# One projection call for the first token mixer, with most of the modulation beside it

## The chip, the cores and the metric

The kernel runs on 1 core of one Trainium2 chip. The metric is the device time of one execution in microseconds. One execution of each kernel is also profiled, and its trace gives the rows shown here. TensorE (PE) multiplies and transposes, VectorE (DVE) and ScalarE (ACT) work elementwise, GpSimd (POOL) does one elementwise job in the part that is changed, and all transfers of this part are issued from one queue, SyncE's (SP).

## The reference, cut to what matters

Two transformer blocks follow each other; the change touches only the first token mixer, up to the residual that follows it. All is float32, with 512 tokens, 256 context tokens and a model width of 1024.

```python
mod = (silu(c) @ w_ada + b_ada)                       # w_ada: 1024 x 6144
sh_mix, sc_mix, g_mix, sh_ffn, sc_ffn, g_ffn = split(mod, 6)
mod_ctx = silu(c_ctx) @ w_ada[:, :2 * d] + b_ada[:2 * d]
h = modulate(rms_norm(x, norm_mix_g), sh_mix, sc_mix)
p_in = h @ w_in + b_in                                # w_in: 1024 x 5824
u = gelu(p_in[..., U]); v = gelu(p_in[..., V])
tq = axial_rope(p_in[..., TQ]); tk = axial_rope(p_in[..., TK]); tv = p_in[..., TV]
nq, nk, nv = ...                                      # 16 heads of 32
gate_a = sigmoid(p_in[..., GA]); gate_b = sigmoid(p_in[..., GB])
hc = modulate(rms_norm(ctx, norm_mix_g), mod_ctx[:d], mod_ctx[d:])
# the context's own tk, tv, nk, nv come from hc and the same columns of w_in
tiny = tiny_attention(tq, tk, tv, tk_c, tv_c) @ tiny_w_o
o_a = u * (mix_in_chunks(layer_norm(v)) + tiny)
o_b = neighbourhood_attention(nq, nk, nv, nk_c, nv_c, na_rpb, rows)
merged = gate_a * (o_a @ w_up_a) + gate_b * (o_b @ w_up_b)
x = x + g_mix * (merged @ w_out)
```

## The kernel before, in words

The program is a sequence of blocks (`nc.Block()`): in each, every engine has its own list of instructions, and the next block starts when all engines are through. Within a block, semaphores set the order. There is no planner: the order of the lists is the order of the work. `linked` makes an engine wait for its own last result.

The order is this. `load_constants` brings the identity, the packed columns, two gate rows and `x`. `modulation` multiplies both silu vectors by `w_ada` in 12 blocks of 512 columns (3 buffers; 8 fp32 matmuls with a 512-wide moving operand per block, L208; ScalarE copies the row out, L198), turns the rows into columns, makes the gains and shifts, and spreads the two gate rows over the partitions (L218, L244); one gate row goes to DRAM. `first_mixer` loads `ctx`, norms the 6 row tiles of `x` and `ctx` (`normalise`: squares on ScalarE L266, root, scaling on VectorE L281), turns them into `hT` (`turn`), loads the bias row, and calls `project`.

`project` multiplies in three passes of a split format: each weight block, two buffers, comes in two halves of its rows; ScalarE rounds a half to its high part (L486), VectorE subtracts it for the low part (L500), and TensorE does hi x hi, hi x lo, lo x hi (L452). A unit is one PSUM tile of 24 such matmuls, there are 4 tiles, and each unit is written out by the engine that it names, in order. On VectorE and ScalarE, block b + 1 is halved before the units of block b are written out. SP issues the weights of block b when block b - 2 is done. `side` gives pieces of other work to an engine, placed after the units of a block; before the change only other callers use it.

The first call covers `v`, `tiny` (the small q, k, v), `nq`, `nk` and `nv`, mostly in blocks of 512 columns. Then `joined` adds the halves of `hT` back, since the low half was written over it. The next block prepares: gelu of `v` and its layer norm, the rotations of the small queries and keys, and on GpSimd the bias planes (`near_bias`, L1009, three operations). Then follow a `turn`, `attend` (the tiny attention, four strips), `near_attention` (the windowed attention), a second `project` for `u` (with `hT` halved again), the mixing (`ps_sgu`, L1098 to L1112, whose weights are loaded at its start), a third `project` for both gates in blocks of 256 columns, `merge`, and the output projection with the residual. After that come the experts, the second mixer and the second feed-forward, which the change leaves alone but for where the gate row of the experts' residual is read.

Of the kernel before, what the change touches and what calls it, by code (L numbers as in the profile page):

```python
# [21 lines left out]
P = 128  # L22
# [123 lines left out]
def load_constants(core, a, keep):  # L146

    nc = core.nc
    loads = [(keep["ident"][:], a["k_ident"]), (keep["cols"][:], a["cols"]),
             (keep["gate_mix_row"][:], a["b_gates"][0:D].partition_broadcast(P)),  # L150
             (keep["gate_ffn_row"][:], a["b_gates"][D:2 * D].partition_broadcast(P)),
             (keep["x"][:], a["x"].rearrange("(t p) d -> p t d", p=P))]
    done = core.sig("constants_in")
    with nc.Block() as block:
        @block.sync
        def _(sp):
            for dst, src in loads:
                sp.dma_start(dst, src).then_inc(done.sem, 16)
            sp.wait_ge(done.sem, 16 * len(loads))


def modulation(core, a, keep, scratch):
# [3 lines left out]
    NB, W = 6 * D // W_BLOCK, W_BLOCK  # L166
    w = core.sb("w_ada", [P, 3, KD, W])
    silu_c = core.sb("silu_c", [P, KD, 2])
    rows = core.sb("mod_rows", [2, 6 * D])
    first = core.sb("first_row", [2, P])  # L170
    mod = core.sb("mod", [P, 6 * KD, 2])
    w_in = [core.sig(f"ada_w_{i}") for i in range(3)]
    first_in, c_ready, mm, row_ready = (core.sig(n) for n in ("first_row_in", "silu_c_ready", "ada_mm", "mod_row_ready"))
    turned, row_mm, chain, row_out = (core.sig(n) for n in ("mod_turned", "gain_row_mm", "dve_chain", "gain_row_out"))
    c0 = COLS["c"][0]
    col = keep["cols"]
    with (core.psum("ps_mod_rows", [2, 2, W], F32) as ps, core.psum("ps_mod", [P, 6 * KD, 2], F32) as ps_mod,
          core.psum("ps_row", [P, 2, 2 * W], F32) as ps_row, nc.Block() as block):
        @block.sync
        def _(sp):  # L180
            for b in range(NB):
                if b >= 3:
                    sp.wait_ge(mm.sem, b - 2)
                sp.dma_start(w[:, b % 3], dram_rows(a["w_ada"], b * W, (b + 1) * W)).then_inc(w_in[b % 3].sem, 16)
                if b == 0:
                    sp.dma_start(first[:], a["k_first"]).then_inc(first_in.sem, 16)
            sp.wait_ge(row_out.sem, 4)
            sp.dma_start(scratch["gate_row"], keep["gate_ffn_row"][0:1, :]).then_inc(core.sig("gate_row_kept").sem, 16)

        @block.scalar  # L190
        def _(act):

            for j in range(2):
                nc.scalar.activation(silu_c[:, :, j], col[:, c0 + j * KD:c0 + (j + 1) * KD], ACT.Silu) \
                    .then_inc(c_ready.sem, 1)
            for b in range(NB):
                act.wait_ge(mm.sem, b + 1)
                nc.scalar.activation(rows[:, b * W:(b + 1) * W], ps[:, b % 2, :], ACT.Copy).then_inc(row_ready.sem, 1)  # L198

        @block.tensor  # L200
        def _(pe):
            pe.wait_ge(c_ready.sem, 2)
            for b in range(NB):
                pe.wait_ge(w_in[b % 3].sem, 16 * (b // 3 + 1))
                if b >= 2:
                    pe.wait_ge(row_ready.sem, b - 1)
                for k in range(KD):
                    last = nc.tensor.matmul(ps[:, b % 2, :], silu_c[:, k, :], w[:, b % 3, k, :], start=k == 0,  # L208
                                            stop=k == KD - 1)
                last.then_inc(mm.sem, 1)  # L210
            pe.wait_ge(row_ready.sem, NB)
            for n in range(6 * KD):
                last = nc.tensor.transpose(ps_mod[:, n, :], rows[:, n * P:(n + 1) * P], keep["ident"][0:2, 0:2])
            last.then_inc(turned.sem, 1)
            pe.wait_ge(first_in.sem, 16)
# [2585 lines left out]
```

## Time and profile before

| | us |
|---|---|
| Median of 3 runs | 4338.49 |
| The runs | 4321.89, 4339.66, 4338.49 |
| Profiled execution | 4325.14 |
| Its span in the trace | 4323.4 |
| TensorE, VectorE, ScalarE, GpSimd busy | 3868.5, 2436.8, 1742.3, 682.5 |
| Start of `merge` (its first transfer) | 755.13 |

Times in the trace are microseconds from the start of the span. In a timeline row stand the start, the length, the engine, the line, the operation with its output and inputs and the shape, the count, and in brackets how long the engine had been idle and what ended that. Rows with a count above one are merged. In a table of stretches stand, after start:end, the length, the busy time of TensorE, its weight loads (PEld), VectorE, ScalarE and GpSimd with their numbers of instructions, the clock granted to TensorE (1.00 is 2.4 GHz, 0.50 is 1.2), and the busy share and rate of DMA. An fp32 matmul of the program is two records.

### The profile page before, as it was taken

The numbers are of one execution on the slowest core, as the hardware profiler recorded it, in microseconds if no ns is written. First come the engines' busy times: TensorE is split into PE (matmuls) and PEld (weight loads), VectorE is DVE, ScalarE is ACT, GpSimd is POOL, SyncE is SP. The second block draws the span as 40 slices with busy tenths as digits, with TensorE's granted clock in tenths as the row PEclk, the third lists the DMA queues.
The fourth block names the chain that finished last, engine by engine and source line by source line (L and its number), as shares of the span: only waits on it lengthen the run. The fifth ranks groups of instructions, "written<-read, shape, count | busy, mean of one in ns | idle before, by whom it ended". The sixth has DMA issues, their size and how long they took to land. (4 is left out here: it accounts for less than half of the span.)

```text
span 4323.4 us, 46785 instructions
## 1 busy us (share of the span) xinstructions
PE 3868.5 (89%) x18351; PEld 3127.2 (72%) x18351; DVE 2436.8 (56%) x3808; ACT 1742.3 (40%) x2078; POOL 682.5 (16%) x390
## 2 busy tenths in 40 slices
PE   7694989867999999993987998799999999999999
PEld 1583867645878887882876766688888887888887
DVE  0326422546888888884336653499666643444444
ACT  0222422224888888883222331333333332222222
POOL 0002000003766776750000000000000000000000
PEclk9795779978999999995998879899999999999999
DMA  7211012224777777772212102244455455555554
GB/s 263 72 49 41 1 51 78 97 113 162 251 243 252 253 255 259 247 255 92 80 50 64 39 25 75 82 137 132 132 180 195 180 195 181 195 193 192 192 192 174
DMA packets 253046, 640.03 MB, mean 148 GB/s; under 512 B 48455, under 2 KB 147531, under 8 KB 209820
## 3 DMA queue, kind: packets, MB, share of 16 engines
q1 hardware_dynamic: 208460, 598.02, 39.4%
q0 software_dynamic: 44368, 39.01, 4.2%
q8 instruction: 147, 2.41, 0.2%
q14 instruction: 71, 0.58, 0.0%
HBM read 671.93 MB, written 125.33 MB: 184 GB/s over the span
## 5 line engine op out<-in xcount | busy, mean ns | idle before, releaser
L1541 DVE TENSOR_TENSOR w_lo<-w_raw,w_hi 128x2048 fp32r<-128x2048 f32 x288 | 653.3, 2290 | 122.8 <-ACT w_hi L1450 113.6
L1450 ACT ACTIVATE w_hi<-w_raw 128x2048 fp32r<-128x2048 f32 x288 | 544.2, 1920 | 65.7 <-DMA w_raw<-in_e_w,over_rows 62.4
L2450 DVE TENSOR_TENSOR w_lo<-w_raw,w_hi 128x2048 fp32r<-128x2048 f32 x128 | 293.4, 2293 | 351.5 <-ACT w_hi L2387 351.0
L2387 ACT ACTIVATE w_hi<-w_raw 128x2048 fp32r<-128x2048 f32 x128 | 245.5, 1918 | 522.1 <-DMA w_raw<-in_peer_u 275.4
L1165 PE MATMUL ps_peer<-peer_xT_hi,w_hi 128*128 128x512 f32 x1024 | 408.3, 399 | 5.0 <-DVE w_lo L2450 4.8
L1165 PE MATMUL ps_peer<-w_hi,coef_hi 128*128 128x512 f32 x1024 | 399.3, 390 | 5.2 <-DVE coef_lo L2547 5.2
L1167 PE MATMUL ps_peer<-peer_xT_hi,w_lo 128*128 128x512 f32 x1024 | 399.5, 390 | 0.0
L1166 PE MATMUL ps_peer<-peer_xT_lo,w_hi 128*128 128x512 f32 x1024 | 399.5, 390 | 0.0
L1166 PE MATMUL ps_peer<-w_lo,coef_hi 128*128 128x512 f32 x1024 | 399.1, 390 | 0.0
L1167 PE MATMUL ps_peer<-w_hi,coef_lo 128*128 128x512 f32 x1024 | 399.1, 390 | 0.0
L1681 PE MATMUL ps_gu<-w_hi,h2T_hi 128*128 128x512 f32 x792 | 321.4, 406 | 0.7 <-DVE w_lo L1541 0.7
L1683 PE MATMUL ps_gu<-w_hi,h2T_lo 128*128 128x512 f32 x792 | 313.0, 395 | 0.0
L1682 PE MATMUL ps_gu<-w_lo,h2T_hi 128*128 128x512 f32 x792 | 312.8, 395 | 0.0
L486 ACT ACTIVATE w_hi<-w 128x1024 fp32r<-128x1024 f32 (+5 forms) x116 | 145.3, 1259 | 377.7 <-DMA w<-in_w_in 257.7
L500 DVE TENSOR_TENSOR w_lo<-w,w_hi 128x1024 fp32r<-128x1024 f32 (+5 forms) x116 | 169.6, 1473 | 214.1 <-ACT w_hi L486 213.6
L1414 POOL DMA_INDIRECT expert_rows<-block_out,slot_token x95 | 214.9, 2262 | 131.0 <-ACT block_out L1470 62.0
L1165 PEld LDWEIGHTS ps_peer<-w_hi,coef_hi 128*128 128x128 f32 x1024 | 192.7, 188 | 45.7 <-issue 5.6
L1165 PEld LDWEIGHTS ps_peer<-peer_xT_hi,w_hi 128*128 128x128 f32 x1024 | 192.9, 188 | 43.9 <-DVE w_lo L2450 6.2
L1167 PEld LDWEIGHTS ps_peer<-peer_xT_hi,w_lo 128*128 128x128 f32 x1024 | 192.6, 188 | 40.7
L1166 PEld LDWEIGHTS ps_peer<-w_lo,coef_hi 128*128 128x128 f32 x1024 | 192.8, 188 | 40.1
L1167 PEld LDWEIGHTS ps_peer<-w_hi,coef_lo 128*128 128x128 f32 x1024 | 192.6, 188 | 40.0
L1166 PEld LDWEIGHTS ps_peer<-peer_xT_lo,w_hi 128*128 128x128 f32 x1024 | 193.0, 188 | 37.8
(487 smaller groups left out, 7736.4 us busy)
## 6 DMA issues: line engine op xcount, KB each, us to landing
w_raw<-in_e_w SPq DMA_DIRECT2D x195, 1024.0 KB
w_raw<-in_peer_u SPq DMA_DIRECT2D x64, 1024.0 KB, 5.9
w_raw<-in_peer_v SPq DMA_DIRECT2D x64, 1024.0 KB, 4.9
acts<-act_out SPq DMA_DIRECT2D x64, 512.0 KB, 6.6
gates<-gate_tile SPq DMA_DIRECT2D x8, 4096.0 KB, 15.9
act_back<-acts SPq DMA_DIRECT2D x64, 512.0 KB, 5.8
gates_back<-gates SPq DMA_DIRECT2D x64, 512.0 KB, 7.0
w<-in_w_in SPq DMA_DIRECT2D x26, 1024.0 KB, 7.3
```

The lines of the kernel that those rows point to most:

```text
L500: nc.vector.tensor_tensor(half_of(w_lo, b, half), half_of(w, b, half), half_of(w_hi, b, half).bitcast(F32), ALU.subtract) \
L1165: nc.tensor.matmul(out, w_hi, x_hi, start=first, stop=False)
L1166: nc.tensor.matmul(out, w_hi, x_lo, start=False, stop=False)
L1167: return nc.tensor.matmul(out, w_lo, x_hi, start=False, stop=last)
L1414: nc.gpsimd.indirect_dma_start(out=scratch["expert_rows"], out_offset=bass.IndirectOffsetOnAxis(ap=tok[:, r:r + 1], axis=0), in_=ob[:, b % ...
L1450: nc.scalar.activation(w_hi[:, slot(n), :], w_raw[:, slot(n), :], ACT.Copy).then_inc(hi_done.sem, 1)
L1541: nc.vector.tensor_tensor(w_lo[:, slot(n), :], w_raw[:, slot(n), :], w_hi[:, slot(n), :].bitcast(F32), ALU.subtract).then_inc(lo_done.sem, 1)
L1681: nc.tensor.matmul(out, s_hi, m_hi, start=first, stop=False)
L1682: nc.tensor.matmul(out, s_hi, m_lo, start=False, stop=False)
L1683: return nc.tensor.matmul(out, s_lo, m_hi, start=False, stop=last)
L2387: nc.scalar.activation(w_hi[:, n % 2, :], w[:, n % 2, :], ACT.Copy).then_inc(w_hi_done.sem, 1)
L2450: nc.vector.tensor_tensor(w_lo[:, n % 2, :], w[:, n % 2, :], w_hi[:, n % 2, :].bitcast(F32), ALU.subtract) \
```

## The change

- `front` replaces `load_constants`, `modulation` and the norms: SP issues the columns, then the first four blocks of `w_ada` (shifts and scales of the mixer) with `x`, the identity and `ctx` between them, each block into its own buffer. The squares and scalings stand between the row copies. Only 16 columns are turned.
- The other eight blocks of `w_ada` become 32 late steps, side work of the projection: VectorE multiplies two 128x512 pieces of `w_ada` by the silu column of their rows and adds them up in SBUF; after four steps TensorE sums over the partitions with four small matmuls against ones. The gates leave as columns, are turned, and go through DRAM to become rows.
- One call of `project` with 23 blocks, nearly all 256 columns wide: `v` 0 to 3, `tiny` 4, `nk` 5 and 6, `nv` 7 and 8, `nq` 9 and 10, `u` 11 to 14, the gates 15 to 22. `joined`, the preparing block and two of the three calls are gone. Gelu, layer norm and rotations are side pieces.
- Transfers: the first `turn` issues bias row, table and layer norm's bias; the second issues `near_mask` and `raw_bias` ahead of what follows; `near_attention` issues the mixing's weights; `x` is dropped after the first turn and loaded again beside the mixing.
- GpSimd makes the bias planes beside the tiny attention (`attend`) instead of beside the layer norm.

```diff
+N_EARLY = 4
+N_LATE = 6 * D // W_BLOCK - N_EARLY
+LATE_STEPS = KD // 2
+def front(core, a, keep, ctx, xn, silu_c):
...
+            sp.dma_start(col[:], a["cols"]).then_inc(cols_in.sem, 16)
+            ada(0)
+            sp.dma_start(x[:], a["x"].rearrange("(t p) d -> p t d", p=P)).then_inc(x_in.sem, 16)
+            sp.dma_start(keep["ident"][:], a["k_ident"]).then_inc(ident_in.sem, 16)
+            ada(1)
+            sp.dma_start(ctx[:], a["ctx"].rearrange("(t p) d -> p t d", p=P)).then_inc(ctx_in.sem, 16)
+            for b in range(2, N_EARLY):
+                ada(b)
...
+            row_copy(0)
+            act.wait_ge(x_in.sem, 16)
+            for i in range(TC):
+                if i == T:
+                    row_copy(1)
+                    act.wait_ge(ctx_in.sem, 16)
+                ins = nc.scalar.activation(junk[:], sources[i], ACT.Square, accum_out=stat[:, 0, i:i + 1])
...
+            for b in range(2, N_EARLY):
+                row_copy(b)
...
 def project(core, blocks, halve=(), side=None):
...
                 for half in range(2):
                     sp.dma_start(half_of(w, b, half), half_src(b, half)).then_inc(w_in[b % NW][half].sem, 16)
+                for piece in beside("sp", b):
+                    piece(sp, lambda b: evicted(sp, b))
...
                 last.then_inc(mm.sem, 1)
+                if n == len(units) - 1 or units[n + 1][0] != b:
+                    for piece in beside("pe", b):
+                        piece(pe, lambda b: evicted(pe, b))
...
 def attend(core, tiles, dv, outs, beside=None):
...
+        @block.gpsimd
+        def _(pool):
+            if beside:
+                beside(pool)
...
+    def fetch_late(i):
+        def piece(sp, ready):
+            b, k = divmod(i, LATE_STEPS)
+            if i >= 2:
+                sp.wait_ge(late_used.sem, i - 1)
+            at = (N_EARLY + b) * W_BLOCK
+            sp.dma_start(w_late[:, i % 2], dram_rows(a["w_ada"], at, at + W_BLOCK)[:, 2 * k:2 * k + 2]) \
+                .then_inc(late_in[i % 2].sem, 16)
+        return piece
+
+    def add_late(i):
+        def piece(dve, link, ready):
+            b, k = divmod(i, LATE_STEPS)
+            dve.wait_ge(late_in[i % 2].sem, 16 * (i // 2 + 1))
+            if k == 0 and b >= 2:
+                dve.wait_ge(late_mm.sem, b - 1)
...
+            for j in range(2):
+                src, by, to = w_late[:, i % 2, j, :], silu_c[:, 2 * k + j, 0:1], acc[b % 2][:]
+                if k == 0 and j == 0:
+                    ins = nc.vector.tensor_scalar(to, src, by, None, ALU.mult)
+                else:
+                    ins = nc.vector.scalar_tensor_tensor(to, src, by, to, ALU.mult, ALU.add)
+                if j == 0:
+                    link(ins)
+            ins.then_inc(late_used.sem, 1)
+            dve.wait_ge(late_used.sem, i + 1)
+        return piece
+
+    def sum_late(b):
+        def piece(pe, ready):
+            pe.wait_ge(late_used.sem, LATE_STEPS * (b + 1))
+            for c in range(W_BLOCK // P):
+                last = nc.tensor.matmul(ps_late[:, b * (W_BLOCK // P) + c, :], acc[b % 2][:, c * P:(c + 1) * P], ones[:],
+                                        start=True, stop=True)
+            last.then_inc(late_mm.sem, 1)
+        return piece
...
+    FIRST = 3
+    side = {"sp": {}, "act": {}, "dve": {}, "pe": {}}
+    for i in range(N_LATE * LATE_STEPS):
+        b = FIRST + i // 2
+        side["sp"].setdefault(b + 1, []).append(fetch_late(i))
+        side["dve"].setdefault(b, []).append(add_late(i))
+        if i % LATE_STEPS == LATE_STEPS - 1:
+            side["pe"][b + 1] = [sum_late(i // LATE_STEPS)]
+    side["sp"][7].append(fetch_gain)
+    side["act"][5] = [gelu_rows(t) for t in range(T)]
+    side["act"][9] = [ln_root]
+    for b, pieces in ((5, [tiny_rope(t, 0) for t in range(T)]), (6, [tiny_rope(t, TINY) for t in range(T)]),
+                      (7, [ln_moments(0), ln_moments(1)]), (8, [ln_moments(2), ln_moments(3)]),
+                      (11, [ln_centre(0), ln_centre(1)]), (12, [ln_centre(2), ln_centre(3)]),
+                      (13, [ln_gained(0), ln_gained(1)]), (14, [ln_gained(2), ln_gained(3)]),
+                      (15, [ln_shifted(0), ln_shifted(1)]), (16, [ln_shifted(2), ln_shifted(3)])):
+        side["dve"][b] += pieces
+    side["dve"][21] = [late_out]
+    with core.psum("ps_late", [P, 4 * KD, 2], F32) as ps_late:
+        project(core, blocks, [h], side)
...
+    def fetch_bias(sp):
+        sp.dma_start(mask[:], a["k_near_mask"]).then_inc(raw_in.sem, 16)
+        sp.dma_start(raw[:], a["k_rpb"]).then_inc(raw_in.sem, 16)
...
+    near_attention(core, nq, nk, nv, near_bias, onT, fetch_mixing)
...
         @block.sync
         def _(sp):
-            sp.dma_start(ws[:], a["sgu_w"]).then_inc(in_.sem, 16)
-            sp.dma_start(wo[:], a["tiny_w_o"]).then_inc(in_.sem, 16)
-            sp.dma_start(bs[:], a["sgu_b"].partition_broadcast(P)).then_inc(in_.sem, 16)
+            sp.wait_ge(rows_kept.sem, 16)
+            sp.dma_start(x[:], a["x"].rearrange("(t p) d -> p t d", p=P)).then_inc(x_in.sem, 16)
+            sp.dma_start(gate_mix_row[:], scratch["gate_rows"][0].partition_broadcast(P)).then_inc(x_in.sem, 16)
+            sp.wait_ge(x_in.sem, 32)
```

## Rows read from the trace of the kernel before

**Rows 1.** Stages: start:end, length, PE, PEld, DVE, ACT, POOL busy, clock, DMA, GB/s.

```profile
0.00:122.30 122.30, 96.60 (x248) 22.95 (x248) 3.92 (x12) 8.64 (x15) 0.20 (x4) 0.95 0.67 233
122.30:154.60 32.30, 8.50 (x48) 7.98 (x48) 10.80 (x17) 13.13 (x23) 0.00 (x0) 0.61 0.15 52
154.60:320.40 165.80, 153.11 (x816) 133.01 (x816) 43.48 (x38) 40.06 (x36) 0.00 (x0) 0.94 0.20 69
320.40:374.10 53.70, 0.00 (x0) 0.00 (x0) 46.77 (x78) 6.67 (x7) 22.57 (x4) 0.54 0.20 81
374.10:383.40 9.30, 6.77 (x38) 6.26 (x39) 3.17 (x5) 3.01 (x6) 0.00 (x0) 0.73 0.00 0
383.40:408.20 24.80, 21.27 (x100) 14.13 (x101) 11.72 (x40) 7.66 (x21) 0.00 (x0) 0.79 0.00 0
408.20:559.90 151.70, 147.88 (x1040) 128.08 (x1040) 68.41 (x172) 65.68 (x160) 0.00 (x0) 0.74 0.00 1
559.90:616.80 56.90, 45.34 (x192) 37.11 (x192) 16.03 (x12) 20.34 (x21) 0.00 (x0) 0.88 0.21 74
616.80:658.10 41.30, 32.13 (x80) 18.23 (x80) 11.13 (x16) 0.00 (x0) 0.00 (x0) 0.52 0.12 32
658.10:755.10 97.00, 89.55 (x384) 73.62 (x384) 19.61 (x16) 28.63 (x33) 0.00 (x0) 0.94 0.28 87
```

**Rows 2.** Whom TensorE waited for, 0 to 755 us: total, times, longest.

```profile
PE ps_turn L314 <- PEq L995: 54.5, 1, 54.5
PE ps_unit L452 <- DVE w_lo L500: 34.8, 3, 15.0
```

**Rows 3.** Timeline of TensorE, modulation and first turn.

```profile
21.70 85.48 PE L208 MATMUL ps_mod_rows<-w_ada,silu_c 128*2 128x512 f32 x192 [21.70 <-DMA w_ada<-in_w_ada]
141.36 8.53 PE L314 MATMUL ps_turn<-ident,xn 128*128 128x128 f32 x48 [22.37 <-PEq L260]
```

**Rows 4.** DMA issues: KB each, median us to landing.

```profile
w_ada<-in_w_ada SPq DMA_DIRECT2D x12, 2048.0 KB, 8.0
raw_bias<-in_k_rpb SPq DMA_DIRECT2D x1, 3072.0 KB, 11.5
```

**Rows 5.** Timeline of VectorE and ScalarE, evictions of the first projection.

```profile
184.41 0.69 DVE L942 TENSOR_TENSOR v<-ps_unit,b_rows 128x512 f32<-128x512 f32 x1 [4.75 <-PE ps_unit L452]
231.14 0.36 DVE L942 TENSOR_TENSOR tiny_qkv<-ps_unit,b_rows 128x192 f32<-128x192 f32 x1 [2.97 <-PE ps_unit L452]
266.75 1.23 ACT L967 ACTIVATE nk<-ps_unit,cols 128x512 f32<-128x512 f32 x1 [2.61 <-PE ps_unit L452]
269.62 0.48 ACT L948 ACTIVATE nk<-ps_unit,cols 128x256 f32<-128x256 f32 x1 [1.64 <-PE ps_unit L452]
```

**Rows 6.** Timeline of VectorE and ScalarE, gate blocks and start of merge.

```profile
695.47 1.22 DVE L500 TENSOR_TENSOR w_lo<-w,w_hi 128x1024 fp32r<-128x1024 f32 x1 [0.21 <-ACT w_hi L486]
699.79 0.69 ACT L948 ACTIVATE gate_a<-ps_unit,cols 128x512 f32<-128x512 f32 x1 [3.78 <-PE ps_unit L452]
760.65 2.50 DVE L494 TENSOR_TENSOR x_lo<-near_outT,x_hi 128x512 fp32r<-128x512 f32 x4
```

**Rows 7.** Timeline of TensorE, windowed attention.

```profile
486.19 1.04 PE L813 MATMUL ps_o<-nv,probsT 128*128 128x32 f32 x8
```

**Rows 8.** Timeline of VectorE and GpSimd, layer norm beside the bias planes.

```profile
346.98 0.60 DVE L1038 TENSOR_SCALAR ln_stats<-ln_stats 128x4 f32<-128x4 f32 x1
348.08 7.29 DVE L1043 TENSOR_SCALAR v<-v,ln_stats 128x1024 f32<-128x1024 f32 x1
L1009 POOL TENSOR_TENSOR near_bias<-near_mask,raw_bias x3: 7287/7296/7737, 340.3 to 354.8; 128x4096 f32<-128x4096 f32 x3
```

**Rows 9.** Timeline of VectorE, tiny attention.

```profile
386.05 0.21 DVE L670 TENSOR_SCALAR maxima<-maxima 128x1 f32<-128x1 f32 x1
```

**Rows 10.** Busy time in two stretches of windowed attention; columns as in rows 1.

```profile
409.90:485.00 75.10, 73.97 (x362) 62.19 (x362) 23.84 (x63) 24.14 (x59) 0.00 (x0) 0.50 0.00 1
556.70:559.90 3.20, 1.11 (x4) 0.71 (x4) 1.95 (x3) 0.00 (x0) 0.00 (x0) 0.50 0.00 0
```

More of the change, by code:

```diff
@@ L155, in _ @@
         @block.sync
         def _(sp):
[L157 to L162, printed above, removed]
-    nc = core.nc
[L166 to L188, printed above, removed]
@@ L286, in normalise, with turn @@
     core.drop(stat, junk)
-def turn(core, jobs, loads=()):
+def turn(core, jobs, loads=(), begin=None):
     nc = core.nc
@@ L300, in _ @@
         def _(sp):
+            if begin:
+                begin(sp)
             for dst, src in loads:
@@ L459, in ready @@
             def ready(b):
[L460 to L462 removed]
+                evicted(eng, b)
             halve_block(0)
@@ L924, in first_mixer @@
-    core.drop(ctx)
+    xn = core.sb("xn", [P, TC, D], high=True)
+    front(core, a, keep, ctx, xn, silu_c)
+    jobs = []
+    for k in range(KD):
+        for first, count, c0, j in ((0, T, 0, 0), (T, CTX // P, S, 1)):
+            jobs.append(([(xn[:, first + i, k * P:(k + 1) * P], i * P) for i in range(count)],
+                         scaled(nc, hT[:, k, c0:c0 + count * P], P, count * P, keep["gain_mix"][:, j, k:k + 1],
+                                keep["shift_mix"][:, j, k:k + 1])))
@@ new lines, in columns, with two @@
+    def columns(at, b, units):
+        blocks.append((dram_rows(a["w_in"], at + b * 256, at + (b + 1) * 256), units))
+    def two(b):
+        return [(j, 2 * b + j) for j in range(2)]
+    scale = NAD ** -0.5
+    for b in range(4):
+        columns(1024, b, [tokens_unit(h, KD, toks(t), 256, "dve", plus_row(v[:, t, b * 256:(b + 1) * 256], b * 256, 256))
+                          for t in range(T)])
+    blocks.append((dram_rows(a["w_in"], 2048, 2240),
+                   [tokens_unit(h, KD, toks(t), 192, "dve", plus_row(tiny[:, t, :], D, 192)) for t in range(TC)]))
@@ new lines, in first_mixer, with gelu_rows, piece @@
+    for name, dst, at, func in (("b_u", u, 0, ACT.Gelu), ("b_ga", ga, 3776, ACT.Sigmoid), ("b_gb", gb, 4800, ACT.Sigmoid)):
+        for b in range(4):
+            columns(at, b, [features_unit(h, KD, j, all_tok, "act", through(func, dst[:, m, :], col(name, m)))
+                            for j, m in two(b)])
+    def gelu_rows(t):
+        def piece(act, link, ready):
+            ready(3)
+            nc.scalar.activation(v[:, t, :], v[:, t, :], ACT.Gelu).then_inc(gelu.sem, 1)
+        return piece
```

377 lines of the change are left out of this document (198 added, 179 removed).

## The prediction

> **What bounds the kernel now.** The page was read first: TensorE is busy 89% of the span, but its row of tenths has holes in the first quarter, and the rows by stage show where [rows 1]. Up to 755 us the program is ten stages, each closed off from the next. In the four that project (154.6 to 320.4, 559.9 to 616.8, 658.1 to 755.1, and the modulation before 122.3) TensorE is nearly always busy, so they end when its matmuls end. In 122.3 to 154.6 it works 8.5 of 32.3 us, in 320.4 to 374.1 not at all. The waits say the same: one wait of 54.5 us before the turn at 374, and three of 34.8 us in all for the first low half of a weight block, one at each projection's start [rows 2]. The chain that ended last lies in the stages after 755 and is untouched: what the change gives is the shift of the moment at which `merge` starts, 755.1 now.
>
> **Front.** The modulation's 12 blocks of `w_ada` took 85.48 us on TensorE, from 21.70 [rows 3]. That is 7.12 a block; the clock was low at the start (the stage's mean is 0.95 [rows 1]), which twelve blocks shared and four now carry alone, an estimate of 2 us more. Four remain: 28.5 + 2 = 30.5. The first `w_ada` is issued at about 1.2 instead of 13.6 us. A 2048 KB block took 8.0 us to land with others beside it [rows 4], so it is there at about 8; with `x` and `ctx` between the blocks I allow 2.4 us more of waiting: matmuls end at 41. The last row copy, 16 small transposes and five small VectorE operations: 43.9. If the 11.6 MB went no faster than 2.1 MB in 8.0 us, the last half block would land at 46 and the front end at 51; if they never held TensorE, 42. The norms (ScalarE busy 13.1 us and VectorE 10.8 in the second stage, turn included [rows 1]) lie beside 30 us of matmuls that need neither engine but for four row copies: nothing on the path. With the cover gone they would cost the 13 us that they cost now.
>
> The turn that follows keeps its 8.5 us [rows 3], with a us for its edges: 9.5. Its three loads (1.2 MB) land within it; the separate load of the bias row (3.8 of the 32.3 us) goes. The projection starts at 43.9 + 9.5 = 53.4, against 154.6.
>
> **The one projection.** Start: `hT` is halved as before; the blocks are half as wide, so ScalarE's and VectorE's first pieces are 1.06 and 1.23 us instead of twice that: 9.3 us to the first matmul, against 10.3. Then TensorE's units, each timed by its evictions [rows 5]: 5.44 us with 512 columns, 3.33 with 192, 2.87 with 256 (1.64 idle behind 1.23). The `v` blocks now have 256 columns: 16 x 2.87 = 45.9 (8 x 5.44 = 43.5 before). `tiny` 6 x 3.33 = 20.0; keys and values 8 x 8.34 = 66.7; queries 4 x 5.44 = 21.8; `u` 43.5; gates 87.0. Sum 284.9, and 3.0 for the low clock at the start, paid once instead of three times.
>
> Side work on TensorE: eight pieces of four fp32 matmuls with 128x128 weights and 2 columns. The nearest row is the value matmuls with 32 columns, 1.04 us for four [rows 7]: 8 x 1.1 = 8.8. Were the cost by columns alone it would be near 2; were each followed by a drop to the low clock, some 20. I take 8.8, since the weights are the same size and the columns nearly nothing.
>
> Side work on VectorE, 32 late steps over blocks 3 to 18, two to a block: two operations on 128x512 with two SBUF inputs, 0.63 each [rows 6], about 1.35 a step with its waits, 2.7 a block; plus up to 3.4 for rotations or moments, 2.4 for the low halves, under 2.4 for evictions in the query blocks: at most 11 and mostly 6 to 9 of a block of 10.9 us. None of it is on the path: today's gate blocks have the same pace, and there the low half is ready at 696.7 for a block that opens at 699.8 [rows 6]: 3.1 us of slack. The late transfers (1 MB a block) stand behind the next block's weights in SP's queue, not ahead. SP's wait for a used late buffer asks for work of the block that has just ended. Bounds: nothing to 3 us for each of 16 blocks.
>
> The end costs 0.9, one eviction. In all 9.3 + 284.9 + 3.0 + 8.8 + 0.9 = 306.9: it ends at 360.3. The layer norm, the gelu of `v` and the rotations of 320.4 to 374.1 are gone from the path: late next is only the turn.
>
> **Turn and tiny attention.** The turn's stage was 9.3. It now issues `raw_bias` ahead of the `spread` load, 3072 KB that took 11.5 us to land with 1.2 MB ahead [rows 4]. The tiny attention starts only when `spread` is in, so 0 to 3.4 us are added; I take 1.5. GpSimd's three operations, 22.3 us, now start with the tiny attention instead of lying beside VectorE's layer norm. What they did there is in the rows: a VectorE TENSOR_SCALAR of 128x1024 took 7.29 us, up to the end of a GpSimd operation, and one of four elements took 0.60, up to the end of the one before (340.3 + 7.29 = 347.6; it ended at 347.58) [rows 8]. The tiny attention has a TENSOR_SCALAR in each of its four strips (0.21 us [rows 9]), and the exponentials wait for it. If the one-element form is held as the four-element one, strip 0's ends at 7.8 us after the start (2.8 now), strip 1's at 15.1, strip 2's at 24.5 (9.9 now), and from there GpSimd is done: +14.6. If it isn't held, nothing: +0. I take 14.6, the nearest row. So 24.8 + 14.6 = 39.4.
>
> The Trainium skill, SBUF - State Buffer, "Who interferes with whom", adds that a VectorE instruction with two SBUF inputs is held by a GpSimd instruction that reads SBUF. The tiny attention has one such per strip (the sums, L675); if these alone were held, the same walk through the strips gives +6 instead of +14.6. No row here shows such an instruction beside GpSimd. The sum above does not use it.
>
> 360.3 + 9.3 + 1.5 + 39.4 = 410.5.
>
> **Windowed attention, mixing, merge.** Windowed attention: 151.7 as before, its added transfers meet idle DMA (1 GB/s [rows 1]). It ends at 562.2. The stage of `u` (56.9) is gone; its matmuls are counted. Mixing took 41.3 with TensorE busy 32.1; its loads are now in before it starts, 7.4 us less: 33.9. The reload of `x` (2 MB) and the gate row need some 13 us and lie beside it; without cover they would cost that. The granted clock was 0.52 there, and windowed attention ends at 0.50 [rows 10]; TensorE, though always busy, never rose, so I leave it low. The gates' stage (97.0) is gone, counted above. `merge` starts at 562.2 + 33.9 = 596.1 instead of 755.1: -159.0. The profiled execution took 4325.1 us: 4166. The other two runs of the kernel lie 14 us above it, the median 13; I forecast 4170.
>
> Where the 159 come from: front and first turn 101, layer norm stage 54, starts of two projections and wait of mixing 27, fewer starts at the low clock 4; against them 27 for narrower `v` blocks, late pieces, `spread` and contention.
>
> **Rivals.**
> *Mixing at the high clock.* It would follow TensorE work after 3 us instead of 8. For: the clock was 1.0 over most of the second half of windowed attention. Against: it was 0.50 in its last 3 us [rows 10]. The matmuls would take half: -16, 4154. Chance 0.14.
> *No contention in the tiny attention* (+0 or +6 instead of +14.6): -9 to -15, 4157. Chance 0.18.
> *The side work isn't hidden.* For: VectorE has up to 11 us of work in some blocks, all in one order, and DMA carries twice the bytes. If the low half comes 3 us late in each of 16 blocks: +48, 4218. This is also the case in which the change does not do what it says. Chance 0.14.
> *Windowed attention stays at the low clock.* It ran 75.1 us at 0.50 with 362 matmul records, then the other 660 or so at double rate [rows 10]. When it rises depends on what arrives before; never rising costs 660 / 4.82 - 72 = +65, 4235. Rising at once saves 37. Chance 0.06 for the first; the second is inside the range.
> *Slower than before.* TensorE pauses at every block because VectorE's one queue (late step, moments, low half) is longer than a block, and the pauses bring the granted clock to 0.5 for the projection. All 285 us at half rate cost +285; it decides once more than 159 / 285 = 56% of the units run so. All of it: 4455. For: a low clock came after each pause at a stage's edge. Against: the gate blocks had no pause. Chance 0.02.
> The forecast itself: 0.46.
>
> **How the numbers follow.** The first three cases and the forecast hold 0.92 of the chance. Bounds around the forecast: front -2 to +7, late pieces -7 to +11, `spread` -1.5 to +2, tiny attention -15 to 0, windowed attention -37 to +10, run to run 10. The range 4128 to 4212 takes in the forecast, the first two rivals and the lower part of the third; the rest of the third and the last two are what is left out. About 0.5% (20 us) is what a measurement of this kernel tells from no change: faster 0.97, the same 0.01, slower 0.02.
>
> **What would show it.** First fp32r matmul near 63 us, last near 359, with no TensorE gap over 1 us between; low halves ready before each block opens; four-matmul side pieces of 1.1 us; VectorE's TENSOR_SCALAR in the tiny attention at 5 to 7 us while GpSimd runs; mixing beginning within 2 us of windowed attention at clock 0.5; `merge` starting at 596. Gaps before `w_lo` inside the projection, or a tiny attention of 25 us, would make it wrong.

## The result, and the profile after

The changed kernel took 4168.70 us, median of four runs (4162.08 to 4227.19; the longest was a slow execution, which the ratio leaves out, and the median of the other three is 4165.36), against 4337.23 for the kernel before in the same session. The ratio is 0.9614, 95% interval 0.9582 to 0.9645: 3.9% faster. The profiled execution took 4172.05 us, against 4325.1 before: 153.1 us less. The forecast was 4170 (4128 to 4212).

Head of the page after: TensorE is now busy 92% of the span (89% before).

```profile
span 4170.3 us, 47028 instructions
PE 3825.4 (92%) x18440; PEld 3128.0 (75%) x18440; DVE 2465.8 (59%) x3883; ACT 1730.7 (42%) x2075; POOL 688.3 (17%) x390
```

Stages of the changed kernel up to `merge`, with the columns of [rows 1]. In order: front, first turn, start and body of the one projection, second turn, tiny attention, windowed attention, mixing.

```profile
0.00:43.20 43.20, 31.96 (x81) 6.60 (x81) 5.08 (x14) 12.10 (x21) 0.20 (x4) 1.00 0.70 270
43.20:53.20 10.00, 6.19 (x48) 5.06 (x48) 8.09 (x11) 7.36 (x12) 0.00 (x0) 0.98 0.55 169
53.20:354.80 301.60, 294.27 (x1648) 254.96 (x1648) 143.79 (x223) 89.66 (x100) 0.00 (x0) 0.98 0.41 136
354.80:365.20 10.40, 4.64 (x39) 4.14 (x39) 3.84 (x6) 2.54 (x5) 0.00 (x1) 0.91 0.79 307
365.20:399.60 34.40, 28.98 (x104) 18.70 (x104) 23.44 (x40) 7.78 (x21) 22.14 (x4) 0.63 0.00 1
399.60:551.40 151.80, 147.97 (x1040) 127.98 (x1040) 68.39 (x172) 65.44 (x160) 0.00 (x0) 0.74 0.04 10
551.40:585.30 33.90, 32.10 (x80) 18.23 (x80) 11.13 (x16) 0.00 (x0) 0.00 (x0) 0.50 0.21 78
```

Against [rows 1]: the front goes from 122.3 to 43.2; of the stage with the rows' norms and the first turn (32.3) the turn is left, with 10.0; the stages of the layer norm (53.7), of `u` (56.9) and of the gates (97.0) are gone; the projection is one stage, TensorE busy 294.3 of its 301.6 us. `merge` begins at 585.3 instead of 755.1, 169.8 earlier. Its first matmul says the same: 594.79 against 764.43. The span fell by only 153.1, so the stages behind `merge`, which the change doesn't touch, gave 16.7 back.

The front and the first matmul of the projection in TensorE's timeline (start, length, line, what it waited for), against [rows 3]:

```profile
9.36 9.93 PE L230 MATMUL ps_mod_rows<-w_ada,silu_c 128*2 128x512 f32 x16 [9.36 <-DMA w_ada<-in_w_ada]
19.61 7.03 PE L230 MATMUL ps_mod_rows<-w_ada,silu_c 128*2 128x512 f32 x16 [0.33 <-DMA w_ada<-in_w_ada]
27.17 13.89 PE L230 MATMUL ps_mod_rows<-w_ada,silu_c 128*2 128x512 f32 x32 [0.53 <-DMA w_ada<-in_w_ada]
43.17 6.25 PE L329 MATMUL ps_turn<-ident,xn 128*128 128x128 f32 x48 [1.03 <-PEq L172]
59.55 0.55 PE L478 MATMUL ps_unit<-w_hi,hT_hi 128*128 128x256 f32 x1 [10.13 <-DVE w_lo L527]
```

The first block starts when its weights land, at 9.36, and takes 9.93 us where the second takes 7.03. Its first seven matmul records take 1.0 to 1.06 us each, all later ones 0.59, so I read it as the low clock at the start. The clock column can't confirm this: it says 1.00 here, but the first clock record of the trace begins only at 15.2 us, where the durations change. The waits inside the four blocks are 0.3 and 0.5 us.

The side work inside the projection: the eight late pieces on TensorE (instruction durations in ns) and the late steps on VectorE (busy us, mean ns | idle before).

```profile
L1129 PE MATMUL ps_late<-ones,ada_sum_even x32: 165/251/251, 139.3 to 296.6; 128*128 128x2 f32 x32
L1118 DVE SCALAR_TENSOR_TENSOR ada_sum_even<-w_ada,silu_c,ada_sum_even 128x512 f32<-128x512 f32 x28 | 21.0, 751 | 1.2 <-DMA w_ada<-in_w_ada 0.4
L1118 DVE SCALAR_TENSOR_TENSOR ada_sum_odd<-w_ada,silu_c,ada_sum_odd 128x512 f32<-128x512 f32 x28 | 20.9, 747 | 0.8
```

The tiny attention: VectorE's timeline, and GpSimd's three bias operations beside it (these begin at 365.57 and take 7.29 us each).

```profile
369.24 0.21 DVE L702 TENSOR_SCALAR maxima<-maxima 128x1 f32<-128x1 f32 x1
372.99 7.16 DVE L707 TENSOR_TENSOR sums<-sums 128x1 f32<-128x1 f32 x1
382.10 5.31 DVE L707 TENSOR_TENSOR sums<-sums 128x1 f32<-128x1 f32 x1
389.49 0.15 DVE L707 TENSOR_TENSOR sums<-sums 128x1 f32<-128x1 f32 x1
L1193 POOL TENSOR_TENSOR near_bias<-near_mask,raw_bias 128x4096 f32<-128x4096 f32 x3 | 21.8, 7295 | 0.1
```

An addition of two one-column operands takes 0.15 us alone and 7.16 or 5.31 us beside GpSimd. Each held one ends where a GpSimd operation ends: 372.99 + 7.16 = 380.15 and 365.57 + 2 x 7.29 = 380.15; 382.10 + 5.31 = 387.41 and 365.57 + 21.82 = 387.39. The one-element TENSOR_SCALAR keeps its 0.21 us throughout, as in [rows 9].

### The profile page after: what moved, and what is told of

Read it like the earlier page. It is cut to its first block and busy times, and to the rows that moved or that the text cites. A ratio compares the mean times of both kernels' runs of the same rounds, so it can differ in the third digit from the quotient of the medians.

```text
span 4170.3 us, 47028 instructions
## 1 busy us (share of the span) xinstructions
PE 3825.4 (92%) x18440; PEld 3128.0 (75%) x18440; DVE 2465.8 (59%) x3883; ACT 1730.7 (42%) x2075; POOL 688.3 (17%) x390
```

## The experiments

The times of kernels run once are those of the profiled execution, and differences between them are counted from the changed kernel's profiled 4172.05. The kernel before took 4317 to 4353 us over these sessions, so a difference of 10 us between two single executions shows nothing by itself; the stage rows do. Each kernel has one profile.

**Is it the addition of two columns that the tiny attention waits for?** The same sum, written with one tensor operand and one scalar operand:

```diff
+                if G == 1:
+                    link(nc.vector.tensor_scalar(sums[:, 2, cols], sums[:, 0, cols], sums[:, 1, cols], None, ALU.add))
+                else:
                     link(nc.vector.tensor_tensor(sums[:, 2, cols], sums[:, 0, cols], sums[:, 1, cols], ALU.add))
```

> The two-SBUF-input addition of the sums in the tiny attention becomes a one-element TENSOR_SCALAR with the second sum as its pointer operand; all else is the changed kernel. Theory (GpSimd holds a VectorE instruction with two SBUF inputs, and not the one-element TENSOR_SCALAR): no VectorE instruction there takes over 1 us, the stage of the tiny attention falls from 34.4 to 24.8 to 25.5 us, and the kernel is 9 us faster (4160 against 4169) unless the clock of later stages moves. Rival (any small SBUF-to-SBUF VectorE instruction that comes just as a GpSimd operation begins is held): the new instruction takes 5 to 7 us in two strips and the stage stays at 34.

Measured: 4149.05 median (ratio to before 0.9557, 0.953 to 0.9584). Stage windows and the sums in VectorE's timeline:

```profile
365.00:391.60 26.60, 24.29 (x100) 15.40 (x100) 11.93 (x40) 7.64 (x21) 22.13 (x4) 0.71 0.00 1
372.77 0.20 DVE L708 TENSOR_SCALAR sums<-sums 128x1 f32<-128x1 f32 x1
383.21 0.20 DVE L708 TENSOR_SCALAR sums<-sums 128x1 f32<-128x1 f32 x1
```

GpSimd is as busy as before (22.13 us), no sum takes more than 0.20, and the stage is 26.6 instead of 34.4, with VectorE busy 11.9 instead of 23.4. So 7.8 of the 9.6 us that the stage had grown go with this one instruction. The new instruction at 372.77 comes 0.1 us after GpSimd's second operation has begun, the very moment at which the addition was held for 7.16, so the rival is out. The other 1.8 us go with the clock: no other VectorE instruction of the stage is longer than in the kernel before, but the granted clock is 0.71 here and was 0.79 there, and the expected 24.8 to 25.5 was missed by 1.1 us. In the profiled execution a further 16.5 us came from stages that the edit doesn't touch (below).

**What do the late pieces cost TensorE?** Left out:

```diff
-        side["sp"].setdefault(b + 1, []).append(fetch_late(i))
-        side["dve"].setdefault(b, []).append(add_late(i))
-        if i % LATE_STEPS == LATE_STEPS - 1:
-            side["pe"][b + 1] = [sum_late(i // LATE_STEPS)]
```

> Leaves out the late two thirds of the modulation: no late transfers, no late steps on VectorE, no small matmuls; the gates and the experts' gain and shift come from the bias alone. Theory (only the eight groups of small matmuls lie on the path): the stretch from the first fp32r matmul to the last falls from 294.3 to 286 to 287 us. Rival (the side work also delays low halves): it falls by more than 12 us. Second rival (the small matmuls hide behind matmuls in flight): under 3 us.

Measured: from the first matmul of the projection to the first of the turn 287.6 instead of 295.3 us, and to the end of its own last one 286.6 instead of 294.3, as the theory had it: 7.7 us for eight pieces, 0.96 each. The kernel took 4168.69, only 3.4 less. The windowed attention took 163.9 instead of 152.1, since its first 88.2 us ran at clock 0.50:

```profile
391.80:480.00 88.20, 86.54 (x434) 73.47 (x433) 27.93 (x72) 28.20 (x69) 0.00 (x0) 0.50 0.06 16
```

Against that, the experts' stage behind `merge`, from its first matmul to the second mixer, was 6.1 us shorter (1092.3 against 1098.4).

**Is VectorE's side work hidden, and with how much to spare?** Each late step done twice:

```diff
-            for j in range(2):
+            for j in (0, 1, 0, 1):
```

> Each late step does its two VectorE operations twice, so the sums are doubled; transfers and matmuls as before. 2.9 us more of VectorE in each of 16 blocks, 46 us in all. Theory (VectorE has room in every block of 10.9 us): the projection's 294.3 us grow by 0 to 3. Rival (VectorE is near its limit in the blocks with moments, rotations or query evictions): pauses of 1 us and more before low halves, 10 to 46 us in all, and low clock after them.

VectorE in the projection, doubled kernel:

```profile
59.40:354.70 295.30, 294.27 (x1649) 254.97 (x1650) 185.13 (x280) 83.57 (x92) 0.00 (x0) 0.99 0.40 133
```

47.6 us more of VectorE (185.1 against 137.5), and the projection lasts 295.3 as before. So the cover holds with twice the work. This kernel took 4165.35, less than the changed one, though nothing up to `merge` is shorter: see the second mixer's attention below.

**What does it save that the norms lie beside the modulation?** All row copies ahead of the norms in ScalarE's order:

```diff
-            row_copy(0)
+            for b in range(N_EARLY):
+                row_copy(b)
             act.wait_ge(x_in.sem, 16)
...
-            for b in range(2, N_EARLY):
-                row_copy(b)
```

> Undoes one part: the squares of the six row tiles start after the last row copy of the first third of the modulation, so the norms no longer lie beside it. Theory (the norms are hidden at no cost now): the first turn's start moves from 43.2 us to 43.2 + 7.1 for squares + 1.8 for the root + 4.2 for the scaling less the 1.5 of the modulation's own end = 54 to 56. Rival (the norms slow the modulation, through the row copies or the port): 3 us or more come back in the modulation, and the start lies at or below 51.

```profile
55.13 7.61 PE L327 MATMUL ps_turn<-ident,xn 128*128 128x128 f32 x48 [13.23 <-PEq L172]
```

The first transpose came at 55.13 instead of 43.17, behind a wait of TensorE of 13.23 us: the norms cost 12.0 us without their cover, as expected. The turn took 7.61 instead of 6.25: the granted clock is 0.50 in its first 3 us, where it is 1.00 in the changed kernel's. The kernel took 4171.19 all the same, 0.9 less than the changed one. Of the 15.2 us by which its windowed attention begins later, all came back in stages that the edit leaves alone: 5.8 in that attention (146.3 against 152.1, clock 0.78 against 0.74), 5.8 in the experts' stage, 4.7 in the second mixer's attention. So the 12 us are shown by the stage, not by the kernel's time.

**What is the late two thirds' move worth?** All twelve blocks of the modulation in the front, through four buffers, no side work:

```diff
-N_EARLY = 4
+N_EARLY = 12
+N_BUF = 4
```

> Undoes one part: all twelve blocks of the modulation are made in the front, through four buffers, none as side work; the rest is the changed kernel. Theory (TensorE's time with a two-column operand is what the side work saves, and it costs only its small matmuls): the first turn starts at 43.2 + 8 x 6.87 + 2.7 for 32 more small transposes = 101, the projection's stage falls from 295.3 to 287.6, and the kernel is 50 us slower than the changed one (4219 by its 4169), clock of later stages apart. Rival (the front is bound by its transfers, so more blocks cost 5.4 to 8 us each): the first turn starts below 90 or above 107.

Measured: front 100.6 instead of 43.2 (+57.4), projection 288.3 (-7.0), `merge`'s first matmul 646.4 instead of 594.8 (+51.6); kernel 4218.63 (+46.6); the front and the kernel's time were expected at 101 and 4219. The move is worth some 50 us of the 153.

**What was moving the bias planes worth?** The kernel before, with GpSimd's three operations in the tiny attention and nothing else changed:

```diff
-        @block.gpsimd
-        def _(pool):
-            nc.gpsimd.memset(near_bias[:, 3 * NAH], 0.0)
...
+def attend(core, tiles, dv, outs, beside=None):
+        @block.gpsimd
+        def _(pool):
+            if beside:
+                beside(pool)
```

> The kernel before with one part of the change alone: GpSimd's bias planes are made beside the tiny attention instead of beside the layer norm. Theory (the port is held one instruction at a time, either way): the preparing stage falls from 53.7 to 39 to 40 us, since four scalings of 0.7 take the place of 16.4 us, and the tiny attention rises from 24.8 to 33 to 35; the move alone is worth 4 to 5 us. Rival (the tiny attention's longer time in the changed kernel has to do with its buffers or its clock): it stays at 25 and the move is worth 14.

Stage between projection and turn, and tiny attention; then VectorE in both:

```profile
323.00:356.10 33.10, 0.00 (x0) 0.00 (x0) 26.34 (x77) 6.50 (x7) 0.00 (x0) 0.50 0.34 132
364.90:396.10 31.20, 23.18 (x104) 15.53 (x104) 21.51 (x40) 7.63 (x21) 22.10 (x4) 0.78 0.00 0
342.86 0.17 DVE L1033 TENSOR_SCALAR ln_stats<-ln_stats 128x4 f32<-128x4 f32 x1
343.52 2.98 DVE L1038 TENSOR_SCALAR v<-v,ln_stats 128x1024 f32<-128x1024 f32 x4
371.29 1.26 DVE L680 TENSOR_TENSOR sums<-sums 128x1 f32<-128x1 f32 x1
375.62 4.21 DVE L680 TENSOR_TENSOR sums<-sums 128x1 f32<-128x1 f32 x1
381.90 5.18 DVE L680 TENSOR_TENSOR sums<-sums 128x1 f32<-128x1 f32 x1
```

Without GpSimd beside it the four-element TENSOR_SCALAR takes 0.17 us (0.60 in [rows 8]) and the four of 1024 columns 2.98 in all, where one alone took 7.29. The layer norm's stage is 14.4 us shorter (from the projection's first matmul to the turn, 209.2 to 194.8), the tiny attention 6.4 us longer, the windowed attention starts 8.5 us earlier counted from the projection's start. The first stage fell as the theory had it (14.4), the tiny attention grew by less than its 8 to 10, so both expectations missed on the worth of the move: 4 to 5 and 14. Three sums were held, for 1.26, 4.21 and 5.18 us; the first met GpSimd 1.26 us before an end. None of the 8.5 us shows in the kernel's time: 4326.07, against 4325.14 in the profile of the kernel before and 4322.73 in its one execution beside this run. The windowed attention and the stage of `u` behind it took 6.4 us longer (222.4 against 216.1, clock 0.75 against 0.77) and the second mixer's attention 9.6 (131.8 against 122.2).

**Does the clock of the windowed attention depend on what TensorE does in it?** Four added 128x512 fp32 matmuls into a buffer that is overwritten:

```diff
+                for _ in range(4 if n == 1 else 0):
+                    nc.tensor.matmul(ps_pt[:, 1, :], nq[:, 0, 0:P], nk[:, 0, 0:WIDE], start=True, stop=True)
                 for i, at in enumerate(TURNS[j] + (NEAR, NEAR + P)):
```

> The changed kernel with four extra fp32 matmuls of 128x128 weights and 512 columns on TensorE ahead of the second unit of the windowed attention, into a bank that is overwritten right after. Theory (the low clock of the first half is kept by matmuls that use 32 or 64 rows or few columns, and wide full ones lift it, as the modulation's lifted it after 6 us): the clock is 1.00 within 8 us of the stage's start and stays; the stage falls from 152 to about 7 + 112 = 119. Rival (the clock falls again as soon as the extra matmuls end): the stage is 5 to 7 us longer, 157 to 159.

```profile
400.70:410.60 9.90, 8.24 (x33) 4.33 (x33) 3.22 (x9) 2.22 (x6) 0.00 (x0) 0.66 0.51 133
410.60:425.50 14.90, 14.90 (x130) 12.54 (x129) 7.63 (x20) 8.23 (x20) 0.00 (x0) 1.00 0.01 2
425.50:440.30 14.80, 14.80 (x72) 12.39 (x72) 3.82 (x10) 5.41 (x13) 0.00 (x0) 0.52 0.00 1
440.30:453.00 12.70, 12.70 (x64) 10.72 (x64) 4.76 (x12) 3.45 (x9) 0.00 (x0) 0.50 0.00 1
453.00:539.80 86.80, 84.35 (x758) 74.76 (x757) 48.98 (x121) 46.16 (x113) 0.00 (x0) 0.95 0.01 1
```

They lifted the clock within the first stretch (75.1 us at 0.50 in [rows 10]), but it fell back for at least 27 us, with TensorE busy 14.80 of 14.80 and 12.70 of 12.70 us. The stage went from 152.1 to 139.1, between the expected 119 and the rival's 157. The kernel took 4146.63, 25.4 less; 9.7 of that is the second mixer's attention (122.1 against 131.8).

**And the mixing?** Four such matmuls ahead of its first group.

```diff
+            for _ in range(4):
+                nc.tensor.matmul(ps[:, 1, :], ws[:, 0, :], v[:, 0, 0:S], start=True, stop=True)
```

> The changed kernel with the same four extra matmuls ahead of the mixing's first group. Theory (mixing could run at the high clock all along, it only never gets there by itself): from the first mixing matmul to merge's first matmul 43.1 becomes 7 + 17 + 9.2 = 33. Rival (mixing's own matmuls, a quarter to a half of them on 64 rows, let the clock fall again within a few us): 43.1 becomes 46 to 50.

```profile
552.60:576.60 24.00, 22.16 (x88) 12.19 (x88) 11.13 (x16) 0.08 (x1) 0.00 (x0) 0.93 0.30 110
```

The 80 matmuls and the 8 records of the added ones take 24.0 us where the 80 took 33.9; first matmul of mixing to first of `merge` 33.2 instead of 43.1. The kernel took 4152.72: 19.3 less, where the place edited gave 9.9; the second mixer's attention gave another 9.6 (122.2).

**Together, and against the fall.** Three kernels beside each other: the sum and both groups of matmuls; the same with four 96x512 matmuls in the second mixer's attention; the same as the first with two more at each of two later places of the windowed attention.

```diff
+                for _ in range({1: 4, 6: 2, 11: 2}.get(n, 0)):
+                    nc.tensor.matmul(ps_pt[:, n % 2, :], nq[:, 0, 0:P], nk[:, 0, 0:WIDE], start=True, stop=True)
```

> The changed kernel with three edits together: the sum of the softmax sums as a one-column TENSOR_SCALAR in the tiny attention, four added 128x512 fp32 matmuls ahead of the second group of probabilities in the windowed attention, and four at the start of the mixing (their results are overwritten). Theory (each edit has its own place, and what follows depends only on the clock granted there): tiny attention 26.6, windowed attention 133 to 140, mixing to merge 33, and the second mixer's attention at 122 instead of 131.8, so 4172 - 8 - 13 - 10 - 10 = about 4131 in the profiled run. Rival (the clock takes part of it back elsewhere, as it did with the change itself: the windowed attention at 146 or more, or the second mixer's attention at 127 to 137): 4140 to 4150.

> The combination before, and four fp32 matmuls of 96 rows and 512 columns (about 5 us at the low clock, 3 at the high one) ahead of the second unit's turned probabilities in the attention of the second mixer, whose first 65 us run at 0.50 in the kernel before. Theory (a short dense stretch lifts the clock, and the work behind it keeps it while its matmuls are short but close): its stage goes from 122 to 90 to 100, the kernel 20 to 30 us faster than the combination. Rival (the clock falls back within some 20 us, as it did in the windowed attention with the added matmuls): stage at 115 to 125, kernel within 8 us of the combination; if it isn't lifted at all, the stage grows by the 5 us added.

> The combination, and two more 128x512 fp32 matmuls each ahead of the seventh and the twelfth group of the windowed attention, in the stretch in which its clock fell back from 1.00 to 0.50 for some 27 us. Theory (the fall is due to what the engine does in the first tile, whose value matmuls use half of the rows, and can be bridged): windowed attention at 120 to 127 instead of 133 to 140, kernel 10 us faster than the combination. Rival (the low clock comes back wherever these matmuls end): stage at 133 to 145, kernel the same or up to 4 us slower.

Measured: 4131.99 (0.9541, 0.9501 to 0.9582), 4130.25 (0.9529, 0.9488 to 0.957) and 4117.22 (0.9517, 0.9453 to 0.9581). The first theory's 4131 was for the profiled run, and that took 4120.83: its stages came out as expected (tiny attention 25.8, windowed attention 139.0, mixing to `merge` 34.4, second mixer's attention 122.0), and the experts' stage, whose code no edit touches, was 11.4 us shorter than in the changed kernel. That the median is 4131.99 is chance. The second is its rival: the clock was at 1.00 for only some 7 us and then back at 0.50, the stage 126.3. In the third the windowed attention took 130.9 us, against 139.0 in the first kernel and 133.2 in the second, which have the same code there. The fall is gone; the clock stays at 1.00 until some 20 us before the stage's end:

```profile
401.30:440.90 39.60, 39.60 (x331) 32.36 (x329) 20.36 (x52) 19.76 (x50) 0.00 (x0) 1.00 0.01 2
440.90:522.40 81.50, 79.06 (x689) 70.12 (x688) 44.74 (x112) 42.32 (x104) 0.00 (x0) 0.92 0.00 1
```

The fall can be bridged, though the stage's 130.9 lies between the theory's 120 to 127 and the rival's 133 to 145. The intervals of the three kernels' times overlap, so that the last 15 us of the median are not shown by the times alone; the profiled executions of the first and the third took 4120.83 and 4120.46, since the experts' stage took 1087.1 and 1104.2. The last kernel adds to the third six such groups in the second mixer's attention:

```diff
+                if U > 8:
+                    for _ in range({1: 4, 4: 2, 7: 2, 10: 2, 13: 2, 16: 2}.get(n, 0)):
+                        nc.tensor.matmul(ps_ptn[:], units[0][2][0], units[-1][2][1], start=True, stop=True)
```

> The combination with the added matmuls at three places of the windowed attention, and in the second mixer's attention four 96x512 fp32 matmuls ahead of the second unit and two each ahead of the fifth, eighth, eleventh, fourteenth and seventeenth, where the single group of four had lifted the clock for some 12 us only. Theory (what bridged the windowed attention bridges this one): its stage goes from 118 to 127 down to about 100 to 108 (the added matmuls cost 12 us of it), the kernel 10 to 20 us faster than with the windowed attention alone: 4097 to 4110. Rival (the clock falls between the groups, since each unit waits for VectorE and ScalarE in turn): stage at 125 to 140, kernel the same or up to 15 us slower.

Measured: 4104.33 (six runs, 4093.89 to 4112.94; ratio to before 0.9477, 0.9451 to 0.9503), so 1.4% below the changed kernel by the ratios; the two intervals don't meet. The stage took 109.3 us (117.6 to 126.3 in the three kernels before it):

```profile
2245.00:2260.00 15.00, 15.00 (x63) 7.60 (x61) 5.20 (x31) 4.38 (x22) 0.00 (x0) 0.85 0.00 2
2260.00:2300.00 40.00, 40.00 (x221) 25.55 (x221) 23.68 (x106) 15.71 (x72) 0.00 (x0) 1.00 0.00 1
```

The stage is shorter though it holds the added matmuls, and the kernel has the lowest median of all, at a mean clock of 0.955 against 0.933. What the last step alone gives the kernel isn't shown by its time: its interval overlaps the third kernel's, and of the 20.2 us between the two profiled executions 16.0 are the experts' stage (1088.1 against 1104.2).

Over all profiles the effect of the added matmuls in their own stages stands clear. In the seven kernels derived from the changed one or equal to it that have none in the windowed attention, that stage took 146.2 to 163.9 us, in the five that have them 130.9 to 139.1. Mixing to `merge` took 43.1 in all seven without them and 33.2 to 34.4 in the five with them. Which property of these matmuls does it (width, rows, or just the denser work) was not tried.

## Why the prediction was right, and where it wasn't

By its own steps, forecast against profile:

- Front: 43.9 against 43.2. The first block's weights landed at 9.4, not 8; the low clock at the start cost 2.9 us (9.93 against 7.03), not 2; the waits between the blocks were 0.9, not 2.4. The reason given for the low start, a stage mean of 0.95, was misread: in the kernel before the clock column is at 1.00 until some 104 us and low only at the stage's end. The slow start shows in the durations of the first seven matmul records alone.
- First turn and start of the projection: first matmul at 62.7 against 59.5. The turn's transposes took 6.25 us, not 8.5 [rows 3]: I had kept a duration that contained a start at the low clock. Here TensorE came to them 1.0 us after the modulation, there after 22.37 us; with a wait of 13.23 us put back, they took 7.61.
- Projection: 296.7 from first to last matmul against 294.3. The late pieces were 7.7 us, not 8.8; VectorE's late operations 0.75 us, not 0.63 (the 0.63 was a mean of four run together; one addition of that shape alone takes 0.69), and hidden all the same, even twice over. From 59.55 to the turn at 354.84 TensorE was busy 294.3 of 295.3 us; the rest is the 1.0 us before the turn.
- Turn with `raw_bias` ahead of `spread`: 10.8 against 10.4.
- Tiny attention: 39.4 against 34.4. This step failed in its mechanism. I took the one-element TENSOR_SCALAR as held like the four-element one; it isn't (0.21 us). What is held is the addition of two SBUF columns. The Trainium skill, SBUF — State Buffer, "Who interferes with whom", says this of instructions with two SBUF inputs; the trace agrees (7.16 and 5.31 us beside GpSimd, 0.15 alone). It gave +6 by my walk; the stage grew by 9.6, of which 7.8 went away with that instruction. The walk took the strips at the clock of the kernel before, 0.79; the stage now ran at 0.63, and TensorE's busy time rose from 21.3 to 29.0 us.
- Windowed attention 151.7 against 151.8, mixing 33.9 at the low clock against 33.9 at 0.50.

Up to `merge` this sums to 596.1 against 585.3: 10.8 us better than forecast, 5.5 of it by the end of the projection, 5.0 in the tiny attention. From there the step that failed is "what the change gives is the shift of the moment at which `merge` starts". The experts and the second mixer behind it gave 16.7 back. 4325.1 - 169.8 + 16.7 = 4172.0: the two misses nearly cancel. The prediction's last step doesn't follow from its own numbers either: it puts the median 13 us above the profiled run and then adds 4 to 4166, without a reason. With all 13 it would have said 4179; the changed kernel's median was 3.4 below its profiled execution. So the total is right by more luck than its 2 us suggest.

Where the 16.7 lie: the largest part is the attention of the second mixer, the same matmuls of the same code (some 512 records in either profile). The last stretch at the low clock and the next, in the kernel before and in the changed one:

```profile
2482.60:2507.20 24.60, 24.60 (x87) 16.10 (x86) 9.69 (x44) 6.24 (x30) 0.00 (x0) 0.50 0.00 1
2507.20:2515.40 8.20, 8.20 (x29) 5.32 (x28) 3.87 (x15) 1.88 (x8) 0.00 (x0) 0.50 0.00 0
2515.40:2523.60 8.20, 8.20 (x50) 5.54 (x49) 4.52 (x19) 2.83 (x14) 0.00 (x0) 0.97 0.01 2
```

```profile
2344.10:2368.70 24.60, 24.60 (x84) 16.04 (x82) 9.90 (x37) 5.57 (x25) 0.00 (x0) 0.50 0.00 0
2368.70:2376.90 8.20, 8.20 (x38) 5.36 (x37) 3.76 (x15) 1.72 (x7) 0.00 (x0) 0.69 0.01 2
2376.90:2418.50 41.60, 31.50 (x192) 20.94 (x193) 27.93 (x84) 19.98 (x61) 0.00 (x0) 0.91 0.09 26
```

The stage begins at 2449.8 and 2286.7. The clock rises 65.6 us in before, over 82 us in after: 122.2 us against 131.8, so 9.6 of the 16.7; the rest is scattered (+4.3 from the first turn behind `merge` to the second mixer, +2.5 from there to its attention, others of either sign). It is no effect of the change itself: the kernel with the doubled late steps, alike in everything from the second turn on, had 122.2 again, the kernel before with only the bias planes moved had 131.8, and the same stage took 127.0 and 136.6 with the norms last and with all blocks early. Which of these a kernel gets, and whether it is the kernel or the single execution that gets it, was not settled by any run, since no kernel was profiled twice. What is shown is that this stage's length goes with the granted clock (mean 0.70 where it took 122.2, 0.65 where it took 131.8), and that the kernel with added matmuls throughout had it at 109.3.

The experts' stage between the two mixers varies by more. From its first matmul to the second mixer it took 1087.1 to 1104.2 us in the fourteen profiles, at a mean clock of 0.94 each time, though no edit touches its code; what makes these 17 us stays open. So a single profile's saving is to be trusted to some 10 to 20 us here, unless it is read stage by stage: of e.g. the 24.3 us that the rewritten sum gained in its profile, 7.8 are its own, 5.9 and 9.6 came from the windowed attention and the second mixer's attention. The medians (4149.05 and, without the longest execution, 4165.36) differ by 16.3, but the intervals of the two ratios still touch (0.953 to 0.9584, 0.9582 to 0.9645), so the times alone don't show the gain.

Worth of the parts, where a run isolates one: late two thirds of the modulation some 50 us, norms beside the modulation 12, the bias planes' move 8.5 in the kernel before, the last two by the stages alone. In the changed kernel, where the layer norm is side work, that move puts 7.8 us of contention on the path. No run takes back the layer norm as side work or the merging of the three projections; for those there are only the stages that are gone.

## What to carry to other kernels

Work that only needs an engine with slack is free if it is cut into pieces of each block's size and placed in that engine's order so that what the bound engine waits for next is still ready in time; price the pieces that must run on the bound engine (0.96 us for four tiny matmuls here) and treat the rest as zero. A GpSimd operation of several us should not lie beside a dependent chain in which VectorE adds two SBUF operands, however small: write that addition with a scalar operand. And after any change up front, compare length and granted clock of the stages that weren't touched before crediting or blaming the change.

## What the runs showed of the hardware

TensorE busy in nearly every us still ran at 0.50: 73.97 of 75.10 us in [rows 10], 12.70 of 12.70 in the kernel with four added matmuls, 32.10 of 33.90 in the mixing. The Trainium skill, TensorE: Matmul & The Clock Gate, "What's actually happening", ties the low level to idleness and the high one to sustained activity; these stretches show that a busy share near 1 in the profile isn't enough for the high level. A few wide fp32 matmuls lifted it and, repeated, kept it at 1.00 for some 100 us of the windowed attention. These are all that the last kernel adds to the two attentions (busy us, mean ns), 10.1 and 15.9 us of TensorE's time:

```profile
L845 PE MATMUL ps_pt<-nk,nq 128*128 128x512 f32 x16 | 10.1, 781 | 0.0
L644 PE MATMUL ps_ptn<-mla_kT,mla_qT 96*128 96x512 f32 x28 | 15.9, 705 | 0.3 <-ACT probs L756 0.3
```

A VectorE instruction that is held by GpSimd ends with GpSimd's instruction, not a fixed time later: 1.26, 4.21, 5.18, 5.31 and 7.16 us for the same 0.15 us addition. Of the TENSOR_SCALARs, those of 4 and of 1024 columns were lengthened beside GpSimd (0.17 to 0.60, some 0.75 to 7.29), those of one column never (0.20 and 0.21).
